# Moving eight more tokens of an expert layer from dense tiles to gathered rows, with weights loaded in pairs of tiles

## What is computed

```python
q = (xf @ w_query).reshape(t, PEER_HEADS, 2, HALF_QUERY)
scores = jnp.einsum('thpk,hpnk->thpn', q, sub_keys)
v1, i1 = lax.top_k(scores[:, :, 0], PEER_TOPK)          # 8 heads, 128 keys, 16 kept
v2, i2 = lax.top_k(scores[:, :, 1], PEER_TOPK)
best, pos = lax.top_k(v1[..., :, None] + v2[..., None, :], PEER_TOPK)
experts = e1 * N_KEYS + e2                               # 128 experts per token
gates = jax.nn.softmax(best, axis=-1)
a = gelu(einsum('cd,ced->ce', x, expert_u[experts])) * gates
out = einsum('ce,ced->cd', a, expert_v[experts])
```

## Time and profile before

| | |
|---|---|
| median of 3 runs | 1619.54 us (1618.03 to 1620.83) |
| the profiled execution | 1618.06 us, span 1616.2 us |
| TensorE busy | 1607.6 us (99%) |
| VectorE busy | 1281.6 us (79%) |
| ScalarE busy | 690.6 us (43%) |
| GpSimd busy | 370.1 us (23%) |
| moved by DMA | 424.34 MB, mean 263 GB/s |
| u tiles | from 521 to 1084 us |
| V tiles | from 1088 us to the end |

### The profile page before, as it was taken

The page is one execution under the profiler, slowest core; times in us unless marked ns, Lnnn a source line. Parts: engine busy times, 40 slices in busy tenths (PEclk is TensorE's granted clock), DMA queues, the critical chain, the costliest instruction groups (busy, mean ns, idle before and its releaser), DMA issues.

```text
span 1616.2 us, 25174 instructions
## 1 busy us (share of the span) xinstructions
PE 1607.6 (99%) x8581; PEld 1422.9 (88%) x8581; DVE 1281.6 (79%) x2311; ACT 690.6 (43%) x921; POOL 370.1 (23%) x286
## 2 busy tenths in 40 slices
PE   9999999999999999999999999999999999999998
PEld 7888888888888999999999999998888888888887
DVE  6855733335457999998999998778898999998997
ACT  5323423333325433334666766433334333333333
POOL 0000000000000100003222222433453445554551
PEclk9999999999999999999999999999999999999999
DMA  4322332222321655658899999998999999999994
GB/s 170 131 93 97 116 109 91 94 100 94 115 81 64 224 185 194 212 191 334 318 367 364 377 359 374 403 376 324 387 413 367 402 414 398 403 415 393 414 378 161
DMA packets 126919, 424.34 MB, mean 263 GB/s; under 512 B 16384, under 2 KB 19472, under 8 KB 125200
## 3 DMA queue, kind: packets, MB, share of 16 engines
q1 hardware_dynamic: 75168, 232.85, 39.3%
q0 software_dynamic: 39264, 142.64, 23.0%
q10 hardware_dynamic: 12432, 48.26, 7.6%
HBM read 375.18 MB, written 48.51 MB: 262 GB/s over the span
## 4 chain that ended last, share of the span: by engine, by line
PE 99%; DMA 0%; DVE 0%; ACT 0%; SPq 0%; issue 0%; ACTq 0%
PE bank L922 21%; PE bank L923 20%; PE bank L924 20%; PE bank L1104 11%; PE bank L1106 11%; PE bank L1105 11%; PE bank L1082 3%; PE bank L988 1%; DMA w_raw<-w_in 0%; PE bank L968 0%; PE bank L967 0%; PE bank L969 0%; PE bank L1118 0%; DVE u_lo L1203 0%; PE bank L1039 0%; PE bank L940 0%
## 5 line engine op out<-in xcount | busy, mean ns | idle before, releaser
L1157 DVE TENSOR_TENSOR w_lo<-w_raw,w_hi 128x1024 fp32r<-128x1024 f32 x347 | 423.4, 1220 | 147.3 <-ACT w_hi L589 142.3
L589 ACT ACTIVATE w_hi<-w_raw 128x1024 fp32r<-128x1024 f32 x347 | 366.3, 1057 | 353.2 <-PE bank L1106 214.9
L922 PE MATMUL bank<-xn_hi,w_hi 128*128 128x368 f32 (+1 forms) x1472 | 516.6, 351 | 0.1
L924 PE MATMUL bank<-xn_hi,w_lo 128*128 128x368 f32 (+1 forms) x1472 | 510.7, 347 | 0.0
L923 PE MATMUL bank<-xn_lo,w_hi 128*128 128x368 f32 (+1 forms) x1472 | 510.6, 347 | 0.0
L538 POOL DMA_INDIRECT rows<-u_rows,expert x128 | 156.0, 1218 | 958.5 <-DVE expert L1558 544.4
L1104 PE MATMUL bank<-w_hi,a_hi 128*128 128x512 f32 x768 | 298.9, 389 | 0.0
L1106 PE MATMUL bank<-w_hi,a_lo 128*128 128x512 f32 x768 | 298.8, 389 | 0.0
L1105 PE MATMUL bank<-w_lo,a_hi 128*128 128x512 f32 x768 | 298.8, 389 | 0.0
L922 PEld LDWEIGHTS bank<-xn_hi,w_hi 128*128 128x128 f32 x1472 | 276.2, 188 | 17.8 <-issue 0.6
L924 PEld LDWEIGHTS bank<-xn_hi,w_lo 128*128 128x128 f32 x1472 | 276.1, 188 | 17.6
(11 more groups left out here) (225 smaller groups left out, 1381.7 us busy)
## 6 DMA issues: line engine op xcount, KB each, us to landing
w_raw<-u SPq DMA_DIRECT2D x128, 512.0 KB
w_raw<-v SPq DMA_DIRECT2D x128, 512.0 KB
g_dram<-g_sb ACTq DMA_DIRECT2D x12, 2048.0 KB, 10.6
g_in<-g_dram SPq DMA_DIRECT2D x84, 256.0 KB
act_dram<-act_out ACTq DMA_DIRECT2D x54, 384.0 KB
act_in<-act_dram SPq DMA_DIRECT2D x54, 384.0 KB
w_raw<-gate SPq DMA_DIRECT2D x32, 512.0 KB
w_raw<-w_in SPq DMA_DIRECT2D x31, 512.0 KB
```

Source lines behind the costliest of these rows:

```text
L589: act.activation(w_hi[:, slot, :], w_raw[:, slot, :], ACT.Copy).then_inc(hi_done, 1)
L922: pe.matmul(out, hi, x_hi, start=k == 0, stop=False)
L924: last = pe.matmul(out, lo, x_hi, start=False, stop=k == NB - 1)
L1157: dve.tensor_tensor(w_lo[:, slot, :], w_raw[:, slot, :], w_hi[:, slot, :].bitcast(F32), ALU.subtract).then_inc(lo_done, 1)
```

## The change

- `EXTRA` goes from 16 to 24: u tiles are 360 columns wide, 8 more `u` rows are gathered and dotted (152 instead of 144), a third group of tokens is laid out, turned on TensorE (8 transposes) and kept in `scratch`. The three-part masks now cover the last 32 tokens (`EXTRA_SPAN`), from mask 22 on (`EXTRA_MASK`), of which 8 tokens have plain gates; `extra_gates` runs before mask 22 and has one instruction more.
- `DOTS_ROUND` has 10 dots instead of 9, `DOTS_PLAIN` 8 instead of 7: 10 dots more before the V part, which has 42 left instead of 44.
- `KEPT_STEPS` is 6: step 26 is kept on chip beside the dense columns of `xn`, in two activations per tile.
- `extra_t` is loaded in 6 parts of 4 tokens, one ahead of each of the first six activations of the fifth round, instead of in one part ahead of that round.
- Weights of `u` and `v` are loaded two tiles at a time, 1 MB, after the `w_lo` that frees the second slot. In DRAM `u` holds two tiles side by side; `v` and `u_rows` are ordered by the first key, with 129 rows per key.

```diff
-EXTRA = 16
+EXTRA = 24
+EXTRA_LOAD = 4
+EXTRA_BANK = (6, 4, 6)
+ROW_STEP = KEYS + 1
-DOTS_ROUND = (1, 1, 1, 1, 1, 1, 1, 2)
-DOTS_PLAIN = (2, 2, 1, 2)
+DOTS_ROUND = (1, 1, 1, 2, 1, 1, 1, 2)
+DOTS_PLAIN = (2, 2, 2, 2)
+EXTRA_MASK = (DT - EXTRA) // MASKED
+EXTRA_SPAN = DT - MASKED * EXTRA_MASK
-KEPT_STEPS = 5
+KEPT_STEPS = 6
+KEPT_J = DT // P
...
+            def load_pair(source, n, slot):
+
+                sp.wait_ge(lo_done, n + 1 - SLOTS + 1)
+                sp.dma_start(w_raw[:, slot:slot + 2, :].rearrange("p s d -> p (s d)"), source
+                             ).then_inc(raw_loaded[slot], 16)
...
-            load_all(u_d, AT_U, KEYS - N_PIECES)
+            for b in range(SLOTS):
+                sp.wait_ge(lo_done, AT_U + b - SLOTS + 1)
+                sp.dma_start(w_raw[:, b, :], u_d[b // 2, :, b % 2, :]).then_inc(raw_loaded[b], 16)
+            with sp.Fori(1, (KEYS - N_PIECES) // SLOTS) as i:
+                for b in range(0, SLOTS, 2):
+                    load_pair(u_d[ds(SLOTS // 2 * i + b // 2), :, :, :].rearrange("o p s d -> (o p) (s d)"),
+                              SLOTS * i + (AT_U + b), b)
...
-                load_raw(u_d, e2, AT_U + e2, e2 % SLOTS)
+                if e2 % 2 == 0:
+                    load_pair(u_d[e2 // 2].rearrange("p s d -> p (s d)"), AT_U + e2, e2 % SLOTS)
                 load_g(0, piece)
...
-                    load_raw(v_d, e2 + b, SLOTS * g + (AT_V + b), b)
+                    if b % 2 == 0:
+                        load_pair(v_d[:, e2 + b:e2 + b + 2, :].rearrange("p s d -> p (s d)"), SLOTS * g + (AT_V + b), b)
...
+            def load_extra(k):
+
+                tokens = slice(EXTRA_LOAD * k, EXTRA_LOAD * (k + 1))
+                act.dma_start(extra_t[:, tokens], extra_dram[tokens, :].rearrange("t p -> p t"),
+                              allow_slow_non_contiguous=True).then_inc(extra_loaded, 16)
...
             def g_round(s, last=False):
                 for b in range(ROUND * SLOTS):
+                    if isinstance(s, int) and s == ROUNDS - 2 and b < EXTRA // EXTRA_LOAD:
+                        load_extra(b)
                     gelu_tile(ROUND * s + (ONEHOT_AT + b // SLOTS), b % SLOTS)
...
-            act.dma_start(extra_t[:], extra_dram.rearrange("t p -> p t"), allow_slow_non_contiguous=True
-                          ).then_inc(extra_loaded, 16)
             g_round(ROUNDS - 2)
...
+                    elif b == 1:
+                        pe.wait_ge(x_tok_ready, 2)
                     else:
-                        pe.wait_ge(x_tok_ready, 2)
+                        pe.wait_ge(x_extra_ready, 2)
                     turn_extra(b)
...
-                        if last_round and q >= GROUPS_PER_ROUND - SLOTS:
-                            held, parts = masks_x, EXTRA_PARTS
+                        if last_round and q // SLOTS >= EXTRA_MASK % MASKS_PER_ROUND:
+                            held, parts = masks_x[q // 4 % 2], EXTRA_PARTS
...
-                    if n == DT // MASKED - 1 and b % 2 == 0:
+                    if n == EXTRA_MASK and b % 2 == 0:
                         extra_gates()
...
+def by_first_key(w):
+
+    return np.concatenate([w.reshape(KEYS, KEYS, D), np.zeros((KEYS, ROW_STEP - KEYS, D), np.float32)], 1)
...
-        "u": a["expert_u"][0].reshape(KEYS, KEYS, NB, P).transpose(1, 3, 2, 0).reshape(KEYS, P, D),
-        "v": a["expert_v"][0].reshape(KEYS, KEYS, D).transpose(1, 0, 2),
-        "u_rows": a["expert_u"][0].reshape(KEYS, KEYS, D).transpose(1, 0, 2),
+        "u": a["expert_u"][0].reshape(KEYS, KEYS // 2, 2, NB, P).transpose(1, 4, 2, 3, 0).reshape(KEYS // 2, P, 2, D),
+        "v": by_first_key(a["expert_v"][0]),
+        "u_rows": by_first_key(a["expert_u"][0]),
```

More of the change, by code:

```diff
@@ L581, in root, with split_weight @@
                 act.activation(stat[:, 1, :], stat[:, 0, :], ACT.Sqrt).then_inc(root_ready, 1)
-            def split_weight(n, slot, times):
-                act.wait_ge(raw_loaded[slot], 16 * times)
+            def split_weight(n, slot, times, pairs=False):
+                act.wait_ge(raw_loaded[slot - slot % 2 if pairs else slot], 16 * times)
                 if not isinstance(n, int) or n >= SLOTS:
@@ L742, in gelu_tile @@
                     to = kept_at(step - (U_STEPS - KEPT_STEPS), b)
[L743 to L747, removed]
+                if not stored and step == U_STEPS - KEPT_STEPS:
+                    whole = KEPT_J - 1
+                    act.activation(to[:, whole, DU - whole * P:], ones[:, 0:EXTRA], ACT.Copy).then_inc(ones_set, 1)
+                    act.activation(to[:, 0:whole, :], bank[b][:, GT:GT + whole * P].rearrange("p (j t) -> p j t", t=P),
+                                   ACT.Gelu).then_inc(ones_set, 1)
+                    act.wait_ge(ones_set, 2 * b + 3)
+                    act.activation(to[:, whole, 0:DU - whole * P], bank[b][:, GT + whole * P:T - EXTRA], ACT.Gelu
+                                   ).then_inc(act_ready, 1)
+                else:
+                    if not stored and step < U_STEPS - 1:
+                        act.activation(to[:, DU:], ones[:, 0:EXTRA], ACT.Copy).then_inc(ones_set, 1)
+                        act.wait_ge(ones_set, SLOTS * (step - (U_STEPS - KEPT_STEPS) + 1) + b + 2)
+                    act.activation(to[:, 0:DU], bank[b][:, DENSE], ACT.Gelu).then_inc(act_ready, 1)
+                split_weight(SLOTS * step + (AT_U + SLOTS + b), b, step + (AT_U // SLOTS + 2), pairs=True)
                 if stored and b % 2 == 1:
@@ L1618, in extra_gates @@
             def extra_gates():
-                last = slice(DT - EXTRA, DT)
-                dve.wait_ge(extra_loaded, 16)
-                chain.did(dve.scalar_tensor_tensor(gate_t[:, last], gate_t[:, last], 1.0 / GATE_SCALE, extra_t[:],
+                last, plain, extra = slice(DT - EXTRA_SPAN, DT), slice(DT - EXTRA_SPAN, DT - EXTRA), slice(DT - EXTRA, DT)
+                dve.wait_ge(extra_loaded, 16 * EXTRA // EXTRA_LOAD)
+                chain.did(dve.scalar_tensor_tensor(gate_t[:, extra], gate_t[:, extra], 1.0 / GATE_SCALE, extra_t[:],
                                                    ALU.mult, ALU.mult))
+                chain.did(dve.tensor_single_scalar(gate_t[:, plain], gate_t[:, plain], 1.0 / GATE_SCALE, ALU.mult))
                 chain.wait()
```

69 lines of the change are left out of this document (41 added, 28 removed).

## The result

The change makes the kernel **slower**: 1643.58 us, median of 4 runs (1641.07 to 1649.73), against 1619.17 (4 runs of the kernel before on the same chip, 1618.03 to 1620.83). The ratio is 1.0156, 95% interval 1.0123 to 1.0188. The prediction was 1615.9, range 1612.6 to 1621.4. The profiled execution took 1641.07 us, span 1639.2.

The account below looks back on a forecast made before the run. TensorE, with 99% of the chain, was taken to bound the kernel. The terms 10.2 - 3.5 + 0.1 - 0.9 - 1.0 - 1.3 = 3.6 us saved gave 1615.9 us for the median, range 1612.6 to 1621.4.

Parts of the forecast that it names:

- Weights in pairs ... Nothing, then, as long as that cover holds: Weight loads: first of each pair asked for one tile (4 us) later; cost nothing, as ScalarE never waits for V-stage loads.
- its own sign of being wrong: The sum is wrong if the V stage shows any TensorE idle; one of three such signs.
- The rival on rows: Plain steps (after the one-hot rounds): late gathered rows leave TensorE standing 6.7 us; 1621.3 us, slower; chance 0.18.
- The plain steps ... a wait of 1.3 us: Steps after the one-hot rounds: eight rows each make VectorE 5.5 us later against 4.2 of distance; TensorE waits 1.3 us.
- Rows starve: Plain steps: at one row per 2.41 us, TensorE stands 6.7 us; 1621.3 us in all; chance 0.18.
- The new order of the tables changes addresses only: Loads from the reordered DRAM tables: no cost in time expected.
- 8 columns are 3.3 ns, a tile 0.08: u matmuls, 368 to 360 columns: 3.3 ns saved per matmul, 0.08 us a tile, 10.2 us over 128 tiles.
- The sixth kept step takes 1.6 MB of stores and as much of loads: DMA traffic: keeping a sixth step on chip removes 1.6 MB of stores and as much of loads.
- top-k swallows its part: Top-k, 560 to 700 us: VectorE has no room, so the first 44 tiles' 3.5 us saves no time.
- 0.9 for the sixteen mask matmuls: Three-part masks covering 32 tokens instead of 16: 16 more matmuls cost TensorE 0.9 us.
- The six loads remove the long hold: Fifth round, ScalarE's queue: extra_t in six loads ends the 5.71 us hold of a store, at no cost.
- A wait of 1.0 us ahead of mask 23: Last one-hot round: added VectorE work outruns 1.5 us of room, so TensorE waits 1.0 us; ends 0 and 3.

Follow-up runs that it names:

- number 10: The changed kernel with single weight loads, the tables of before and 7 dots a plain step: 1614.49 us, ratio 0.9979.
- number 9: The changed kernel with single weight loads and the tables of before, moved dots kept: 1621.72 us, ratio 1.0017.
- number 1: The changed kernel with every u and v weight loaded singly again, changed tables and moved dots kept: 1625.47 us, ratio 1.0036.
- number 11: Number 6 with extra_t loaded in one part ahead of the fifth round instead of six small loads: 1620.41 us, ratio 1.0016.
- number 4: The kernel before with the changed tables alone, each weight still loaded by itself: 1619.67 us, ratio 1.0008.
- number 6: The changed kernel with single weight loads, changed tables and 7 dots a plain step, ten dots a round kept: 1615.49 us, ratio 0.9982.

## Why the prediction was wrong

The ratios in order, each kernel against the one above it, times 1619 us:

| kernel | ratio to before | adds |
|---|---|---|
| 24 tokens, 10 dots a round, six kept steps, six loads (number 10) | 0.9979 | -3.4 us |
| and the eighth dot of a plain step (number 9) | 1.0017 | +6.2 |
| and the changed tables (number 1) | 1.0036 | +3.1 |
| and the pairs (the change) | 1.0156 | +19.4 |

The intervals of the ratios are 0.09 to 0.33% to either side, 1.5 to 5 us, so the +3.1 of the tables is the least certain step.

**"Weights in pairs ... Nothing, then, as long as that cover holds": the step that failed**, 19 us of the 25. I named the cover, ScalarE never waiting for a load in the V stage, and what a lack of it would cost, and then took it to hold. But that row tells how it was with single loads; it says nothing of how much time was left between a landing and its use, and that is what a later request eats. The traces hold the number. The second of two tiles of a pair frees its slot one tile later, 4.0 us. In the kernel before, a weight tile of the plain steps (u117 to u125) landed 3.7 to 4.5 us before ScalarE read it, so a request 4.0 us later leaves nothing; in the changed kernel the pairs of u116 to u124 are read as they land, at 0.0 us. In the V stage the same time was 5.5 us in the median and 2.5 at the least, and is 0.2 in the median with pairs. What is queued behind the pair, `g_in` and above all `act_in`, keeps its order but not its time: `act_in` had 1.4 us in the median before and was waited for 10 times already, and its flight grew by 1.5. That both tiles are whole only when 1 MB is in costs little by these landings. No run parts the late request from the later `act_in` (with `act_in` issued ahead of the pair, say, or with more slots), so how the 19 us divide between them stays open. The forecast also kept the clock at its higher level because nothing idled TensorE long; behind the new waits it was lower, a mean of 0.94 from 1063 to 1083 us. And its own sign of being wrong came: TensorE stands 6.5 us in the V stage. The rival on rows named the right place and the right sign, but its price went by the rows alone.

**"The plain steps ... a wait of 1.3 us": mis-sized.** With single loads and the old tables (number 9) u121 still starts 2.2 us ahead of the kernel before (1054.25 against 1056.41) and the first V tile 3.9 behind it (1091.76 against 1087.83), 6.1 lost, and the eighth dot costs 7.2 us of time by the medians (1621.72 - 1614.49), 6.2 by the ratios. The forecast divided 7.34 MB by the best rate of the trace, 416 GB/s. The rival *Rows starve*, which went by the pace of the rows instead (one per 2.41 us), had 6.7. The pace of the thing that is waited for was the better row here, though it is one case and may be luck: once VectorE waits, the next gather and the next weight are asked for late, and the rate falls (388 GB/s in number 9 from 1023 to 1063 us).

**"The new order of the tables changes addresses only": false**, though it costs only where the plain steps are dry. The rows' flight on the chain is 7.8 to 9.2 us instead of 7.1 to 7.5, and the full DMA engines carry up to 6% less. Which of the two tables read there, `u` or `u_rows`, does it was not tried.

**"8 columns are 3.3 ns, a tile 0.08": too much.** In number 10 u112 starts at 1017.82 and u116 at 1033.61, 3.947 a tile where it was 4.000 (1020.41 to 1036.41). That is 0.053 a tile, and 84 tiles behind u44 give 4.4 us instead of 6.7. The slope from 368 to 512 columns doesn't hold for the step from 368 to 360.

**"The sixth kept step takes 1.6 MB of stores and as much of loads": twice too much.** Two stores and two loads of 384 KB fall away, 0.8 MB each way. The sum didn't use it.

**Right:** top-k swallows its part (u44 moved by the execution's offset alone, 1.05 against 1.00). The sum of what is left fits number 10: 4.4 + 0.1 - 0.9 for the sixteen mask matmuls = 3.6, and its span is 3.5 shorter (1612.7 against 1616.2), though no run shows the 0.9 by itself. The six loads remove the long hold, and number 11 shows their worth, 4.9 us with 24 tokens, which the sum had not counted as at stake. **A wait of 1.0 us ahead of mask 23: not there**; it was ready at 995.95 (its last part starts at 992.46 and takes 3.49 with the two before it) and was used at 996.19, 0.2 us to spare. The forecast's own total without the plain steps' 1.3, a gain of 4.9, came out as 3.5 in number 10: 2.3 too much for the columns, and 1.0 for a wait at the mask that didn't come, partly cancel.

**What stays open:** why pairs in u and in V cost 14.7 us apart and 19.4 together was only argued, by the dry plain steps; and why 8 columns are worth less between 368 and 360 than below.

## What to carry to other kernels

That nobody waits for a load says nothing about how late it may come: before a request is moved or joined to another, take the time from its landing to its first use and compare it with the time by which the request will be later (here 3.7 to 5.5 us against 4.0), and do the same for everything behind it on its queue. Longer runs were the better ones here (pairs in 8 KB runs beat pairs in 4 KB runs), and the pairs still lost 19 us: with four slots they are asked for a tile later, and what is queued behind them lands later. Where an engine already waits for a stream, cost one element more by the pace of that stream and not by the best bandwidth of a window.

## What the runs showed of the hardware

- In the plain steps the same gathers and loads, from tables laid out otherwise (`u_rows` with 129 rows to a key, a u tile's 4 KB pieces 8 KB apart), moved 389 to 392 GB/s in number 4 and 392 to 408 in number 6, instead of 413 to 417, at a busy share of 1.01 to 1.03. In the V stage, with a V tile's 4 KB pieces 516 KB apart, there was no such difference (401 against 399).
- A 1 MB load of two weight tiles landed 7.8 us after its issue in the median of the V stage, a 512 KB load 7.0 to 7.4, with the DMA engines full (the changed kernel; number 1 and the kernel before).
- A 24 x 128 load of single values held the next store on its queue for 10.08 us. The 16 x 128 one held it for 5.71: 1.5 times the elements, 1.8 times the hold. But the store comes 6.6 us behind the load in both; from the issue of the load (923.92 and 926.80) to the end of the hold it is 16.6 us against 12.4, 1.3 times.
- The same 8 columns of a matmul were worth 0.053 us a tile at 368 and 0.08 to 0.09 below 360.
